# A fused encoder layer on one core: the gates of the mixer ahead of its up projections, and the heads' up projection by seven products

## The reference, cut to what matters

```python
z = h @ w_in                      # columns: q | f | i | og | u | ga | gb
o, s_new = hgrn_chunked(q, k, v, logf, s0, chunk)        # 8 heads of 128
o = gnorm(o) * silu(og)
y_a = o @ w_a_up                                         # 1024 x 1024
y_b = (pool_mix(u) * pool_scale) @ w_b_up                # 512 x 1024
m = sigmoid(ga) * y_a + sigmoid(gb) * y_b
x = x + rmsnorm(m @ w_out)
```

## Time and profile before

| | before |
|---|---|
| median of 3 runs | 2333.71 us |
| the profiled execution | 2332.94 us, span 2330.8 us |
| PE busy | 2258.5 us, 97% of the span |
| DVE, ACT, POOL busy | 1514.6, 1283.9, 1339.3 us |
| PE in the chain of waits | 63% |
| HBM read, written | 155.49 MB, 37.88 MB |

### The profile page before, as it was taken

The page is one execution under the profiler, slowest core; times in us unless marked ns, Lnnn a source line. Parts: engine busy times, 40 slices in busy tenths (PEclk is TensorE's granted clock), DMA queues, the critical chain, the costliest instruction groups (busy, mean ns, idle before and its releaser), DMA issues.

```text
span 2330.8 us, 54611 instructions
## 1 busy us (share of the span) xinstructions
PE 2258.5 (97%) x20456; PEld 1935.7 (83%) x20456; DVE 1514.6 (65%) x2563; ACT 1283.9 (55%) x2423; POOL 1339.3 (57%) x1019
## 2 busy tenths in 40 slices
PE   8899999999998999999899999999999999999998
PEld 6788888888887888888778888877888888888786
DVE  7877767635589676667772232398687677445755
ACT  6454555433577677777563433665455455334775
POOL 2777877767614656555644543316778777677120
PEclk9999999999999999999999999999999999999999
DMA  3123222343430111111011112321232223535202
GB/s 133 50 80 103 85 88 86 129 155 115 161 107 20 41 53 45 42 48 59 24 59 41 54 63 81 112 97 37 78 105 77 86 77 93 180 123 194 70 19 75
DMA packets 155246, 195.09 MB, mean 84 GB/s; under 512 B 13168, under 2 KB 102512, under 8 KB 155120
## 3 DMA queue, kind: packets, MB, share of 16 engines
q1 hardware_dynamic: 111920, 153.59, 20.8%
q10 hardware_dynamic: 43200, 39.83, 5.2%
HBM read 155.49 MB, written 37.88 MB: 83 GB/s over the span
## 4 chain that ended last, share of the span: by engine, by line
PE 63%; DVE 12%; POOL 10%; ACT 6%; issue 5%; DMA 3%; SPq 1%; ACTq 0%; POOLq 0%; DVEq 0%
PE bank L1083 16%; PE bank L1086 15%; PE bank L1085 15%; POOL ring L944 5%; PE bank L1050 4%; PE bank L1052 4%; PE bank L1051 4%; DMA ring<-weights 3%; POOL ring L948 3%; DVE hid L2275 2%; DVE ops L2439 1%; DVE hid L2429 1%; DVE ops L2330 1%; DVE ops L2283 1%; POOL wtmp L948 1%
## 5 line engine op out<-in xcount | busy, mean ns | idle before, releaser
L1083 PE MATMUL bank<-ops,ring 128*128 128x264 f16 x4112 | 1139.5, 277 | 23.4 <-DVE ops L2439 8.7
L1085 PE MATMUL bank<-ops,ring 128*128 128x264 f16 x4112 | 1138.8, 277 | 0.0
L1086 PE MATMUL bank<-ops,ring 128*128 128x264 f16 x4112 | 1138.7, 277 | 0.0
L944 POOL TENSOR_TENSOR ring<-ring 128x512 f16<-128x512 f32 (+1 forms) x492 | 644.6, 1330 | 285.2 <-ACT ring L1445 285.2
L1445 ACT ACTIVATE ring<-ring 128x512 f16<-128x512 f32 (+1 forms) x492 | 286.7, 615 | 511.2 <-POOL ring L948 510.4
L1083 PEld LDWEIGHTS bank<-ops,ring 128*128 128x128 f16 x4112 | 403.6, 98 | 95.3 <-DVE ops L2439 10.3
L1086 PEld LDWEIGHTS bank<-ops,ring 128*128 128x128 f16 x4112 | 403.7, 98 | 61.7
L1085 PEld LDWEIGHTS bank<-ops,ring 128*128 128x128 f16 x4112 | 403.7, 98 | 60.4
L929 POOL TENSOR_TENSOR ring<-wtmp,ring 128x512 f16<-128x512 f32 x107 | 132.1, 1239 | 340.5 <-ACT ring L1386 339.9
L1050 PE MATMUL bank<-hid,ring 128*128 128x264 f16 x1068 | 294.9, 276 | 2.5 <-issue 1.3
L1052 PE MATMUL bank<-hid,ring 128*128 128x264 f16 x1068 | 294.8, 276 | 0.0
(11 more groups left out here) (234 smaller groups left out, 3542.4 us busy)
## 6 DMA issues: line engine op xcount, KB each, us to landing
ring<-weights SPq DMA_DIRECT2D x363, 256.0 KB, 2.8
ops<-spill SPq DMA_DIRECT2D x16, 1056.0 KB, 6.6
ring<-weights SPq DMA_DIRECT2D x120, 128.0 KB, 2.5
spill<-hid ACTq DMA_DIRECT2D x42, 264.0 KB, 3.0
spill<-hid ACTq DMA_DIRECT2D x20, 528.0 KB, 5.0
ops<-spill SPq DMA_DIRECT2D x8, 792.0 KB, 4.8
hid<-xT SPq DMA_DIRECT2D x8, 528.0 KB, 8.2
hid<-out_x ACTq DMA_DIRECT2D x8, 528.0 KB, 9.0
```

What stands on the lines that cost most here:

```text
L944: nc.gpsimd.tensor_tensor(low(slot, kh), weight_source(name, k, kh), high(slot, kh), ALU.subtract)\
L1083: nc.tensor.matmul(out, whi, xhi, start=(kk == 0 and fresh(name, k)), stop=False, skip_group_check=True)
L1085: nc.tensor.matmul(out, whi, xlo, start=False, stop=False, skip_group_check=True)
L1086: mm = nc.tensor.matmul(out, wlo, xhi, start=False, stop=end, skip_group_check=True)
```

## The change

The stage `outs` is gone. The 8 `gates` pairs now run one behind the other, with the pooling products in the gaps of pair 1. ACT's sigmoids of each gate row are stored to HBM (`gate_store`, 16 rows of 528 KB). Then 4 times a chained pair `outa` (two tiles of `w_a_up` by seven products, 168 matmuls for what took 192) followed by a turn `outb` (`w_b_up` for the same two tiles, 96 matmuls); SP loads the gates back ahead of each (`load_gates`), and DVE multiplies and adds them. The combinations of the heads' outputs which the seven products need (`ta_*`, four per index kk) are made by DVE and ACT during gates 2 to 6. In the last head the output transposes move one product later, behind the keys' transposes, and `HG_LAST` follows.

```diff
--- before.py
+++ after.py
...
-    "outs": dict(units=3, turns=KD, ks=[KD, 4], kinds="M" * KD, banks=4, bank0=4),
+    "outa": dict(pairs=KD // 2, chained=True),
+    "outb": dict(units=2, turns=KD // 2, ks=[4, 4], kinds="M" * (KD // 2), banks=4, bank0=4),
...
-BESIDE = {"outs": "gates"}
+BESIDE = {"outb": "outa"}
+MIX_UNITS = 7
...
-HG_LAST = (["vT"] * 3 + ["OT"] * 3 + ["kT"] * 3 + ["L32"] * 2 + ["L16"] * 2 + ["D16"] * 2
+HG_LAST = (["vT"] * 3 + ["kT"] * 3 + ["OT"] * 3 + ["L32"] * 2 + ["L16"] * 2 + ["D16"] * 2
...
+        GATE_SETS = (((spare_row(0, 2), spare_row(0, 3)), (spare_row(0, 4), spare_row(1, 2))),
+                     ((spare_row(1, 3), spare_row(1, 4)), (gate_row(0), gate_row(1))))
...
+            def load_gates(p):
+                if p == 0:
+                    b, uses = plan.product("gates", KD - 1, PRODUCTS - 1, 1)
+                    sp.wait_ge(bank_full[b], uses + 1)
+                if p >= 2:
+                    sp.wait_ge(mixed_ready, 1 + 4 * (p - 1))
+                for t in range(2):
+                    sp.wait_ge(gate_stored[t], 16 * (KD if p == 1 else 2 * p + 2))
+                for t in range(2):
+                    for n in range(2):
+                        sp.dma_start(GATE_SETS[p % 2][t][n], gate_store[4 * p + 2 * n + t])\
+                            .then_inc(gates_loaded[p % 2], 16)
...
+                if name == "outa":
+                    for p in range(s["pairs"]):
+                        load_pair(name, p, None if p else last)
+                        for u in range(units_of("outb")):
+                            load("outb", p, u,
+                                 plan.freed_by("outb", p - 1, u) if p else last.get(plan.slot("outb", u)))
+                        if p == 0:
+                            land_wait(name)
+                        load_gates(p)
...
-                    (2, 1): (norms if last else []) + ([] if first else keys),
-                    (3, 1): keys if first else [],
+                    (2, 1): [] if first else keys,
+                    (3, 1): keys if first else norms if last else [],
...
             pair("gates", 0, None, {(1, 1): [lambda: output_transposes(HEADS, HEADS - 1)]})
-            turn("outs", 0, "M", out_rhs, first_out_ready, ts=(0,))
-            turn("pools", 0, "M", pool_rhs, pool_ready, order=POOL_ORDER)
-            turn("outs", 0, "M", out_rhs, first_out_ready, ts=(1,))
-            with pe.Fori(1, KD) as i:
+            pair("gates", 1, None, {(0, 1): [pools(0)], (2, 1): [pools(1)], (4, 1): [pools(2)], (6, 1): [pools(3)]})
+            with pe.Fori(2, KD) as i:
                 pair("gates", i)
-                turn("outs", i, "M", out_rhs)
+            pe.wait_ge(head_ready, HEADS)
+            pe.wait_ge(ta_ready, 4 * KH)
+            pe.wait_ge(mixed_ready, 1)
+            with pe.Fori(0, KD // 2) as i:
+                pair("outa", i, rhs=ta_rhs)
+                turn("outb", i, "M", mix_rhs)
...
+            def gate_turn(m):
+                freed = product_before("gates", m)
...
+                chain_copies("gates", m, 0)
+                if m == 0:
+                    first_highs("gates")(5, 6)
+                    chain_copies("gates", m, 2)
+                    pooled_high(1)
+                    chain_copies("gates", m, 4)
+                    pooled_high(2)
+                    onorm_high(HEADS - 1, W[3])
+                    scale_next()
+                    ahead(0, 1)
+                else:
+                    if m == 1:
+                        mixed_high(0)
+                    if 3 <= m < 3 + KH:
+                        ta_highs(m - 3, 4)
+                    scale_next()
+                    chain_copies("gates", m, 2)
+                    if m == 1:
+                        mixed_high(1)
+                    ahead(0, 1)
+                    chain_copies("gates", m, 4)
+                    if m == 1:
+                        mixed_high(2)
+                    for t in range(2):
+                        act.wait_ge(gate_stored[t], 16 * m)
+                for e in range(2):
+                    b = chained("gates", m, 5, e)
+                    nc.scalar.activation(dst_a[:, (2 * e + 1) * N:(2 * e + 2) * N], bank[b][:, 0:N],
+                                         ACT.Sigmoid, scale=1.0 / WS).then_inc(bank_read[b], 1)
+                sums_read("gates", m, 1)
+                nc.scalar.activation(dst_a.rearrange("p (e s n) -> p e s n", e=2, s=2)[:, :, 0, :],
+                                     ga_even.rearrange("p (e n) -> p e n", e=2), ACT.Sigmoid).then_inc(gate_ready, 1)
+                ahead(2)
+                if 2 <= m < 2 + KH:
+                    ta_highs(m - 2, 1, 2, 3)
+                for e in range(2):
+                    act.wait_ge(bank_read[plan.product("gates", m, 5, e)[0]], plan.product("gates", m, 5, e)[1] + 1)
+                act.wait_ge(gate_ready, 2 * m + 1)
+                act.dma_start(gate_store[2 * m], dst_a).then_inc(gate_stored[0], 16)
+                if m == 0:
+                    pooled_high(3)
+                sums_read("gates", m, 3, 6)
+                nc.scalar.activation(dst_b, gb_all, ACT.Sigmoid).then_inc(gate_ready, 1)
+                ahead(3)
+                if m == 1:
+                    mixed_high(3)
+                ahead(4)
+                act.wait_ge(gate_ready, 2 * m + 2)
+                act.dma_start(gate_store[2 * m + 1], dst_b).then_inc(gate_stored[1], 16)
+                ahead(5, 6)
...
+                chain_copies("outa", i, 0)
+                prep("outb", i, 0, 1)
+                if last:
+                    prep("out0", 0, 0, 1, 2)
+                else:
+                    scale("outa", i + 1)
+                chain_copies("outa", i, 2)
+                ahead(0, 1)
+                chain_copies("outa", i, 4)
+                ahead(2, 3, 4, 5, 6)
+                if last:
+                    prep("out0", 0, 3, 4, 5)
+                for m in (2 * i, 2 * i + 1):
+                    for e in range(2):
+                        act.wait_ge(mix_summed, 2 * m + e + 1)
+                        nc.scalar.activation(mix_tile(m, e, 0), mix_f32(m, e), ACT.Copy).then_inc(mix_high, 1)
...
+            def sums_of(m, *steps):
+                if m:
+                    dve.wait_ge(gate_ready, 2 * m - 1)
+                sums_a("gates", m, lambda g: ga_even[:, g // 2 * N:(g // 2 + 1) * N])
+                steps[0]()
+                if m:
+                    dve.wait_ge(gate_ready, 2 * m)
+                sums_b_odd("gates", m, lambda g: gcols(gb_all, g))
+                steps[1]()
+                sums_b_even("gates", m, lambda g: gcols(gb_all, g))
+                steps[2]()
...
+            def ta_add(kk, n):
+                b12, b22, b21 = head_parts(kk, 0, 1), head_parts(kk, 1, 1), head_parts(kk, 1, 0)
+                first = {1: b12, 2: b22, 3: b22, 4: b21}[n]
+                minus = {1: head_parts(kk, 0, 0), 3: b12}.get(n)
+                t = ta_f32(n)
+                step(V_.tensor_tensor(t, first[0], minus[0] if minus else ta_f32({2: 1, 4: 2}[n]), ALU.subtract))
+                if minus:
+                    step(V_.tensor_tensor(t, t, minus[1], ALU.subtract))
+                V_.tensor_tensor(t, t, first[1], ALU.add).then_inc(ta_summed, 1)
+                dve.wait_ge(ta_summed, 4 * kk + n)
+            def ta_low(kk, n):
+                dve.wait_ge(ta_high, 4 * kk + n)
+                V_.tensor_tensor(ta_split(n, kk, 1), ta_f32(n), ta_split(n, kk, 0), ALU.subtract).then_inc(ta_ready, 1)
...
+                sums_of(0, first_steps, second_steps, lambda: pooled_low(3))
+                mixed_low(0)
+                sums_of(1, lambda: mixed_low(1), lambda: mixed_low(2), lambda: mixed(3))
+                dve.wait_ge(state_stored, 32 * HEADS)
+                dve.wait_ge(head_ready, HEADS)
+                for m in range(2, KD):
+                    kk = m - 2
+                    def blocks():
+                        if 1 <= kk <= KH:
+                            ta_low(kk - 1, 4)
+                        if kk < KH:
+                            for n in (1, 2, 3):
+                                ta_add(kk, n)
+                    def lows():
+                        if kk < KH:
+                            for n in (1, 2, 3):
+                                ta_low(kk, n)
+                            ta_add(kk, 4)
+                    sums_of(m, blocks, lambda: None, lows)
+                for i in range(KD // 2):
+                    outs(i)
...
+                dve.wait_ge(gates_loaded[i % 2], 64 * (i // 2 + 1))
+                own_sums("outa", i, 1)
+                step(V_.tensor_tensor(parity[:, :, 0, :], parity[:, :, 0, :],
+                                      ga_even.rearrange("p (e n) -> p e n", e=2), ALU.mult))
+                sums_b_odd("outa", i, lambda g: gcols(gb_all, g))
...
+                own_sums("outa", i, 3, 6, 5)
+                step(V_.tensor_tensor(ga1, ga1, gb_all, ALU.mult))
```

(44 more changed lines are left out.)

207 lines of the change are left out of this document (97 added, 110 removed).

## The result

| us | before | after |
|---|---|---|
| median of the timed runs | 2332.57 (4 runs, 2331.25 to 2335.29) | 2363.22 (4 runs, 2357.99 to 2371.14) |
| profiled execution | 2332.94 | 2361.74 |
| its span | 2330.8 | 2360.0 |
| mean granted clock | 0.994 | 0.988 |

The changed kernel is slower: the ratio is 1.0133, 95% interval 1.0102 to 1.0164, and the profiled executions lie 28.8 us apart. The prediction was 2353 us with a range of 2331 to 2368, and "slower" with a chance of 0.80.

A forecast was written before the change was run, and what follows sets the result against it. PE, busy for 97% of the span, was taken as the bound: its matmuls plus its few microseconds of waits. The terms summed to +20.3 us on the profiled 2332.9, giving 2353 us, range 2331 to 2368 (forecast's own 2342 to 2362).

The forecast's parts named there:

- waits that go: At the first gates and `outs`, PE's old waits of 1.1, 1.0 and 1.3 us vanish: -3.4 us.
- last head: Keys' transposes no longer wait for `onorm`, no half clock follows, scores start earlier: -6.8 us, ends -7.0 and -2.2.
- start of gates 1, with half clock: PE waits 5.9 us for POOL's first weights, plus 2.3 us of half clock: +8.2 us, ends +5.9 to +9.5.
- product 2 of gates 3 to 7 and `outa` 0: chain: PE waits 2.1 us per pair for ACT's copy behind the weight-making chain, six pairs: +12.6 us, ends +6 and +20.
- DVE beside POOL: At the end of gates 2 to 5, DVE's two-input operations slow POOL's by 1.0 us a pair: +4.0, ends 0 and +10.
- half clock behind the waits: Four gates waits of 3.1 us each lower the granted clock, costing 1.5 us each: +6.0 us, ends 0 and +12.
- product 4 of `outa`: In `outa` 1 to 3, ACT's copy waits behind `scale` for raw weights, 1.9 us each: +6 us, ends 0 and +18.
- Rival E: The last head keeps a wait behind product 3: +4.6 us, 2358 us; chance 0.06.
- Rival A: The chain behind product 6 does not bind, ACT and POOL finishing within 5.4 us: 2321 to 2331 us, faster; chance 0.12.
- Rival B: Small waits come without POOL slowdown or half clock, and `outa` runs free: 2334 to 2337 us; chance 0.10.
- Rival C: DVE holds up each of POOL's three operations behind product 6 by 0.87 us; three more half clocks: 2364 us; chance 0.10.
- Rival D: Gate loads come at half rate, so each `outa` waits 6 us more, three times: 2371 us; chance 0.06.

The follow-up runs named there:

- experiment 1: Kernel before with only the last head's transposes reordered (keys' behind product 2, output behind product 3): 2327.64 us against 2334.25, ratio 0.9969.
- experiment 5: Changed kernel with DVE in gates turns 2 to 5 waiting for POOL's last sum before its lows and fourth sum: 2369.64 us, one run.
- experiment 4: Changed kernel with SP loading the next `outa` pair's raw weights ahead of the gate rows: 2357.56 us, ratio 1.0100 to the kernel before.
- experiments 3 and 4: The first: changed kernel with ACT's copies of product 2 ahead of `scale` in `outa`, 2354.59 us, ratio 1.0099; the second is experiment 4.
- experiment 2: Changed kernel with ACT's copies of the next pair's product 0 ahead of high parts 5 and 6: 2366.09 us, ratio 1.0145 to the kernel before.
- experiment 6: Changed kernel with experiment 2's move, high part 4 behind those copies, product 2's copies ahead of `scale`, one DVE add later: 2337.67 us, ratio 1.0020.

## Why the prediction came out as it did

The direction and the mechanism were right: the product-2 waits, their place, what ends them and their repetition are in the trace. The time was 10 us too low, inside the range of 2331 to 2368 and just over the forecast's own (2342 to 2362). Term by term, in us, from the profiled executions (the first is a count times the pitch; the waits that go are those of the earlier trace rows, none of which the trace after has):

| term | predicted | measured |
|---|---|---|
| 96 matmuls | -10.8 | -10.8 |
| last head | -6.8 | -7.1 |
| waits that go | -3.4 | -3.4 |
| start of gates 1, with half clock | +8.2 | +6.8 |
| product 2 of gates 1, 2 | +4.5 | +3.5 |
| product 2 of gates 3 to 7 and `outa` 0: chain | +12.6 | +12.6 |
| the same: DVE beside POOL | +4.0 | +5.4 |
| half clock behind the waits | +6.0 | +11.1 |
| product 4 of `outa` | +6.0 | +10.6 |
| a sum of DVE late at 1230.45 | 0 | +0.5 |
| sum | +20.3 | +29.2 |

That this sum lies 0.4 us from the 28.8 between the executions is partly luck. From the values' transposes to the first matmul of `out0` the kernel before takes 443.5 us (1106.35 to 1549.88) and the kernel after 473.6 (1107.22 to 1580.78), 30.0 more, of which the terms leave 0.8 unexplained. Outside this stretch, where nothing was changed, the kernel after is 0.9 us later ahead of it and 1.8 us shorter behind it.

- **Last head.** 18.46 less 11.34 is 7.1, and experiment 1 gives it alone. The clock stayed at 1.00 there. Rival E is out.
- **Start of gates 1.** The wait was 4.45 where 5.9 were forecast; the half clock cost 2.3 as borrowed from the last head (some 21 matmuls at 0.22).
- **The chain.** Worked out from the earlier trace rows as 2.1 us and measured as 2.08 and 2.14 where DVE has no combinations to do (1337.25, 1360.13), and as 2.08 in experiment 5 where it was kept away. Rival A, that the chain doesn't bind, is out: the waits are there in six turns. Rival B, that they bring neither slower POOL operations nor half clock, is out by the next two terms.
- **DVE beside POOL.** Here a size was off. The six waits sum to 18.0 (3.07, three times 3.57, 2.08, 2.14), so the company costs 1.48 us in three pairs and 0.97 in one. I had taken one 0.87 us of the earlier trace rows and a little for "the 2 us that overlap"; all three operations of POOL overlapped, each by about 0.5. Rival C had the extent right (each of the three is held up) and the size of each too high, 0.87 for 0.5. It also had three more falls of the clock, as measured, and its 2364 us is the number nearest to the result; that is luck, since its 10.4 us for this term were 5.4 and it had nothing more for `outa`, which took 4.6 more. The Trainium skill (SBUF — State Buffer, "Who interferes with whom") says that a VectorE instruction with two SBUF inputs and a GpSimd instruction that reads SBUF shut each other out for a whole instruction. The rows agree with it in that both sides were stretched, DVE's from 0.71 to 1.6 and POOL's from 1.16 to 1.7.
- **The clock.** The step that failed most. I counted four falls, from the waits over 2.8 us, as if a wait's length told whether the clock falls. There were seven between 1190 and 1500 us: behind the four waits of over 3 us in gates 3 to 6, behind 2.08 us at 1337.25, and behind 3.41 and 3.17 us in `outa`. Some 105 matmuls started 0.22 instead of 0.11 us apart, 11.1 us in all, 1.6 a fall. Two of the three uncounted falls come from the `outa` waits that I had too short; the third stands behind 2.08 us, a length that I had excluded, while behind 2.14 us at 1360.13 the clock stayed at 1.00. The wait of 2.62 us ahead of `out0` is the plainest case. In the kernel before the clock stayed at 1.00 behind it, and from that I had taken 2.6 us for safe; in the kernel after, with the same wait at the same place, it was halved:

```profile
1580.80:1584.00 3.20, 3.20 (x16) 2.22 (x17) 3.10 (x6) 0.76 (x2) 0.69 (x1) 0.52 0.00 0
```

The other way about, it stayed at 1.00 behind 3.24 us in experiment 4. So the length of the last wait alone doesn't decide. What does, no run here shows.
- **`outa`.** The cause was right (experiments 3 and 4), the size not. I had set the first `outa` at nothing because its wait at product 2 should cover it, and it was the longest of the four with 3.41; the others were 1.74, 2.26 and 3.17, and the first and the last brought half clock with them. Why the first is long is read from the DMA issues of the kernel after (xcount, KB each, median us from issue to landing), first from 1352 to 1369 us, then the same for `outa` 1, 1387 to 1402 us, and last SP's and ACT's issues in order of time in `outa` 0:

```profile
ops<-gate_store SPq DMA_DIRECT2D x4, 528.0 KB, 7.8
ring<-weights SPq DMA_DIRECT2D x5, 256.0 KB, 9.2
gate_store<-hid ACTq DMA_DIRECT2D x1, 528.0 KB, 9.0
...
ring<-weights SPq DMA_DIRECT2D x5, 256.0 KB, 7.1
ops<-gate_store SPq DMA_DIRECT2D x2, 528.0 KB, 4.6
hid<-gate_store SPq DMA_DIRECT2D x2, 528.0 KB, 6.6
...
1353.13 1.99 SPq L889 DMA_DIRECT2D ops<-gate_store  x4
1354.36 0.33 ACTq L2211 DMA_DIRECT2D gate_store<-hid  x1
```

ACT issues its last gate store among SP's first gate rows, and it is under way for 9.0 us. The prediction said of stores that "they are done by then". Beside it the rows take 7.8 us instead of 4.6 and 6.6, and the weights behind them 9.2 instead of 7.1 (7.7 in `outa` 2). Rival D, half the rate in every `outa`, is out: in `outa` 1 to 3 the rows take 4.5 to 6.6 us, and even here they don't take twice that. That the store is the cause is argued from the times of the transfers; no run took it away.

## What to carry to other kernels

A chain of small operations on other engines is free as long as PE's turn between two uses is longer than the chain. Before a turn that hid it is taken out (16.2 us here), add up that chain from the trace and compare it with the new distance, because every repetition pays the difference. Before moving one late operation ahead of an engine's wait, list everything else that is queued behind the same wait: experiment 2 moved one consumer and gained nothing, experiment 6 moved both (and two things more) and gained 26 us. A PE wait of 2 to 4 us may bring half clock with it, here 1.6 us a time; put that in the range for every such wait, since its length did not tell which ones brought it.

## What was not expected of the hardware

- The granted clock fell to 0.62 behind a wait of 2.08 us and stayed at 1.00 behind one of 2.14 us, 23 us later. Behind the same wait of 2.62 us it stayed at 1.00 in the kernel before and was 0.52 in the kernel after, and behind 3.24 us in experiment 4 it stayed at 1.00.
- DVE and POOL operations with two inputs take turns: 528 columns on DVE go from 0.71 to 1.54 and 1.66 us, 512 columns on POOL from 1.16 to 1.62 and 1.73, and return to 1.16 when DVE is held back (experiment 5).
- With one store of 528 KB from ACT's queue under way, 256 KB loads of SP's queue took 9.2 us in the median from issue to landing, and 7.1 and 7.7 in the next two `outa` without one. That the store is the cause no run shows.
